# Head outputs return inside the last attention head, and the w_b and w_out stages are entered row by row (gMLP + latent attention + expert-choice block, one core)

## The reference

```
p = rmsnorm(x) @ w_in                     # u, v, c_q, c_kv, k_rope, gate_A, gate_B
a_out = chunked spatial gating of u, v, @ w_a_out
b_out = attention(q, k, v of 8 heads) @ w_b_out
x = x + (sigmoid(gate_A) * a_out + sigmoid(gate_B) * b_out) @ w_out
x = x + expert_choice_ffn(rmsnorm(x))     # 16 experts
```

## Time and profile before

| | |
|---|---|
| median of 3 runs | 2310.31 us (2306.19 to 2315.46) |
| the profiled execution | 2310.33 us, span 2308.6 us |
| mean granted TensorE clock | 0.97 of full speed |
| PE busy | 2136.6 us (93% of the span) |
| DVE, ACT, POOL busy | 1212.7, 921.9, 715.9 us |
| w_a tiles 6 and 7 | 759 to 803 us of the span |
| last head of attention | 1115 to 1168 us |
| w_b | 1179 to 1296 us |
| w_out | 1302 to about 1440 us |

### The profile page before, as it was taken

One profiled execution on the slowest core, in us unless ns is written; L12 is line 12 of the kernel. 1 busy time (PEld: TensorE's weight loads), 2 busy tenths in 40 slices (PEclk: granted clock), 3 DMA queues, 4 the chain that ended last, 5 costly groups with the idle time before them and its releaser, 6 DMA issues.

```text
span 2308.6 us, 34507 instructions
## 1 busy us (share of the span) xinstructions
PE 2136.6 (93%) x13812; PEld 1759.1 (76%) x13812; DVE 1212.7 (53%) x1395; ACT 921.9 (40%) x1156; POOL 715.9 (31%) x438
## 2 busy tenths in 40 slices
PE   6999999999989799999969899279999999999996
PEld 5887878888778678888868899257777777777774
DVE  5245402222566367776632413747676767777673
ACT  4112211111544266666520103135555555555552
POOL 3332312123255276666613320211212222122211
PEclk9999999999999999999989999589999999999998
DMA  4121223444567521321143411547888888878873
GB/s 146 53 85 67 93 85 125 142 154 161 197 228 246 191 67 62 91 77 60 34 187 96 157 30 78 214 180 267 291 293 288 287 295 291 294 286 283 296 287 110
DMA packets 189220, 396.85 MB, mean 172 GB/s; under 512 B 16208, under 2 KB 110416, under 8 KB 189136
## 3 DMA queue, kind: packets, MB, share of 16 engines
q1 hardware_dynamic: 176080, 343.25, 41.7%
q0 software_dynamic: 6144, 20.98, 4.2%
q10 hardware_dynamic: 6912, 31.46, 3.4%
HBM read 317.01 MB, written 78.64 MB: 171 GB/s over the span
## 4 chain that ended last, share of the span: by engine, by line
PE 84%; DVE 5%; ACT 3%; DMA 3%; issue 2%; POOL 2%; SPq 1%; ACTq 0%; DVEq 0%; POOLq 0%
PE PS L1229 24%; PE PS L341 13%; PE PS L343 13%; PE PS L342 13%; PE PS L1239 8%; PE PS L1087 2%; PE PS L1074 1%; PE PS L1078 1%; PE PS L1076 1%; PE PS L1075 1%; PE PS L1077 1%; PE PS L1021 1%; PE PS L1184 1%; ACT prob L1525 1%; PE PS L980 1%
## 5 line engine op out<-in xcount | busy, mean ns | idle before, releaser
L341 PE MATMUL PS<-act_hi,w_hi 128*128 128x512 f32 (+1 forms) x1248 | 452.6, 363 | 17.8 <-DVE act_lo L1724 11.2
L343 PE MATMUL PS<-act_hi,w_lo 128*128 128x512 f32 (+1 forms) x1248 | 446.3, 358 | 0.0
L342 PE MATMUL PS<-act_lo,w_hi 128*128 128x512 f32 (+1 forms) x1248 | 446.1, 357 | 0.0
L1983 DVE TENSOR_TENSOR elo<-raw,ehi 128x2048 fp32r<-128x2048 f32 x125 | 283.3, 2287 | 103.4 <-ACT ehi L1590 102.3
L1590 ACT ACTIVATE ehi<-raw 128x2048 fp32r<-128x2048 f32 x128 | 242.0, 1915 | 127.3 <-PE PS L1229 111.2
L341 PEld LDWEIGHTS PS<-act_hi,w_hi 128*128 128x128 f32 x1248 | 238.4, 191 | 51.3 <-issue 13.4
L343 PEld LDWEIGHTS PS<-act_hi,w_lo 128*128 128x128 f32 x1248 | 238.0, 191 | 34.6
L342 PEld LDWEIGHTS PS<-act_lo,w_hi 128*128 128x128 f32 x1248 | 238.5, 191 | 31.9
L785 POOL TENSOR_SCALAR prob<-prob,small 128x1024 f32<-128x1024 f32 (+1 forms) x80 | 196.9, 2462 | 134.4 <-DVE small L1852 134.4
L684 POOL TENSOR_SCALAR w_hi<-w_raw 128x1024 fp32r<-128x1024 f32 x52 | 57.8, 1111 | 500.6 <-PE PS L343 464.3
L835 POOL DMA_INDIRECT y_p<-ob_p,ixs_p x16 | 44.6, 2785 | 454.0 <-DVE ob_s L2027 454.0
(11 more groups left out here) (265 smaller groups left out, 4236.4 us busy)
## 6 DMA issues: line engine op xcount, KB each, us to landing
raw<-in_w_up SPq DMA_DIRECT2D x62, 1024.0 KB, 5.7
raw<-in_w_gate SPq DMA_DIRECT2D x34, 1024.0 KB, 4.9
raw_more<-in_w_down SPq DMA_DIRECT2D x32, 1024.0 KB, 7.6
raw<-in_w_down SPq DMA_DIRECT2D x32, 1024.0 KB, 6.3
raw_more<-in_w_gate SPq DMA_DIRECT2D x30, 1024.0 KB, 5.9
...
```

Of the source, the lines that this page charges most:

```text
L341: pe.matmul(out, lh, rh, start=first, stop=False)
L342: pe.matmul(out, lh, rl, start=False, stop=False)
L343: return pe.matmul(out, ll, rh, start=False, stop=last)
L1983: dve.tensor_tensor(elo[:, pt], raws[slot], f32(ehi[:, pt]), ALU.subtract).then_inc(S["e_lo"], 1)
```

## The change

1. `head_piece`: the first head's 9 pieces start at position 14 of w_a tile 6 instead of 2, and stand 3 instead of 4 positions apart. PE, ACT and DVE follow.
2. `o_all` and `z_all` go; `o_hl` holds both halves of the eight head outputs, in the room of the even heads' buffers. In the last head SP loads one output row a step (`load_o`, from step 71) into the two buffers `stg`, ACT rounds the high half (`o_part`, steps 72 to 77), and DVE subtracts the low half (steps 72 to 77). Rows 6 and 7 follow after step 83, row 7 behind the last pair's store.
3. `b_row`: the products of w_b tile 0 with rows 0 and 1 stand on PE in steps 80 and 81. The other 14 row products of tiles 0 and 1 follow after step 83. Tiles 2 to 7 wait block by block.
4. z tile by tile: SP loads `za_d[i]` into `stg` (`load_za`, in its queue behind the weights of w_b tile i and ahead of those of tile i+1). DVE adds, ACT rounds, and DVE subtracts each row right after its tile (`z_part`); row 0 comes after the gates of tiles 0 and 1.
5. w_out: PE starts with the banks 6 and 7 and takes the rest as they are evacuated. POOL splits the second weight tile in four pieces of two rows each. x is loaded after w_b's last product, since its room is now that of `o_hl`; the weights of the second quarter stand behind it on SP.

The diff, cut to the parts of which the prediction speaks:

```diff
-    q = 24 * (i - 6) + s - 2
-    return q // 4 if q >= 0 and q % 4 == 0 and q // 4 < PIECES else None
+    q = 24 * (i - 6) + s - 14
+    return q // 3 if q >= 0 and q % 3 == 0 and q // 3 < PIECES else None
...
-                o_all = sb(s2, "o_all", [P, KD, T])
-                z_all = sb(s2, "z_all", [P, KD, T])
+                o_hl = sb(s2, "o_hl", [P, KD, 2, T], F32R)
...
+            def load_o(k):
+
+                for r in range(2):
+                    sp.wait_ge(o_st[r], 16 * max(15, (5 * k + 5 + 1 - r) // 2))
+                    if k < 2:
+                        sp.wait_ge(stored[r], 16 * 20)
+                if k > 1:
+                    sp.wait_ge(S["part_lo"], at("part_lo", KD + k - 1))
+                sp.dma_start(stg[:, k % 2, :], o_d[k]).then_inc(ld_in[k % 2], 16)
...
-                if n == STEPS - NCH + 8:
-                    sp.wait_ge(S["scores_pe"], STEPS - NCH + 1)
-                    for r in range(2):
-                        sp.wait_ge(o_st[r], 16 * 15)
-                    sp.dma_start(o_all[:, 0:H - 2], o_d[0:H - 2].rearrange("h p t -> p h t")).then_inc(S["o_back"], 16)
+                if n > STEPS - NCH and n - (STEPS - NCH + 1) < H - 2:
+                    load_o(n - (STEPS - NCH + 1))
+            load_o(H - 2)
             store_values(5 * H - 1)
-            for r in range(2):
-                sp.wait_ge(o_st[r], 16 * 20)
-            sp.wait_ge(S["probT_pe"], STEPS)
-            for h in (H - 2, H - 1):
-                sp.dma_start(o_all[:, h], o_d[h]).then_inc(S["o_back_last"], 16)
+            load_o(H - 1)
...
+            def load_za(i):
+                j = i % 2
+                sp.wait_ge(S["part_lo"], at("part_lo", KD + (i + KD - 1)))
+                sp.dma_start(stg[:, j, :], za_d[i]).then_inc(ld_in[j], 16)
+                if i > 1:
+                    sp.wait_ge(S["z_sum"], at("z_sum", i - 1))
+                    sp.dma_start(gt[:, j, :], g_d[KD + i]).then_inc(gt_in[j], 16)
+
             for j in range(2):
                 sp.wait_ge(stored[j], 16 * 20)
-            for n, (k0, k1) in enumerate(((0, 2), (2, KD))):
-                sp.dma_start(z_all[:, k0:k1], za_d[k0:k1].rearrange("k p t -> p k t")).then_inc(S[f"za_in{n}"], 16)
-            with sp.Fori(1, KD // 2) as i:
-                for j in range(2):
-                    load_w(G_B + 2 * i + j, j, w_tile("b", 2 * i + j))
-                    sp.wait_ge(S["z_sum"], at("z_sum", 2 * i + (j - 1)))
-                    sp.dma_start(gt[:, j, :], g_d[2 * i + (KD + j)]).then_inc(gt_in[j], 16)
-
-
-            sp.wait_ge(S["part_lo"], at("part_lo", 2 * KD))
+            for i in range(2):
+                load_za(i)
+            for i in range(2, KD):
+                load_w(G_B + i, i % 2, w_tile("b", i))
+                load_za(i)
+            for j in range(2):
+                load_w(G_OUT + j, j, w_tile("o", j))
+            sp.wait_ge(S["tile_pe"], 3 * G_OUT)
...
-                    pool.wait_ge(S["part_lo"], at("part_lo", 3 * KD))
+                    pool.wait_ge(S["tile_pe"], 3 * G_OUT)
...
-                    settled()
-                    pool.tensor_scalar(wh[:, j], w_raw[:, j], 1.0, 0.0, ALU.mult, ALU.add).then_inc(S["w_rounded"], 1)
-                    pool.wait_ge(S["w_rounded"], g + 1)
-                    pool.tensor_tensor(wl[:, j], w_raw[:, j], f32(wh[:, j]), ALU.subtract).then_inc(S["w_split"], 1)
+                    for k in (range(0, KD, 2) if g == G_OUT + 1 else (0,)):
+                        ks = slice(k, k + 2) if g == G_OUT + 1 else slice(0, KD)
+                        hi = pool.tensor_scalar(wh[:, j, ks], w_raw[:, j, ks], 1.0, 0.0, ALU.mult, ALU.add)
+                        hi.then_inc(S["w_part"], 1)
+                        pool.wait_ge(S["w_part"], 2 * (q * 2 + j + 1 + (3 if g > G_OUT + 1 else k // 2)) - 1)
+                        pool.tensor_tensor(wl[:, j, ks], w_raw[:, j, ks], f32(wh[:, j, ks]), ALU.subtract)\
+                            .then_inc(S["w_part"], 1)
+                    pool.wait_ge(S["w_part"], 2 * (q * 2 + j + 1 + (3 if g > G_OUT else 0)))
+                    pool.sem_inc(S["w_split"], 1)
...
+            def b_row(j, k):
+
+                if k == 0:
+                    pe.wait_ge(S["w_split"], G_B + j + 1)
+                    pe.wait_ge(S["exp_act"], STEPS)
+                    if j == 1:
+                        pe.wait_ge(S["pt_lo_dve"], STEPS)
+                pe.wait_ge(S["part_lo"], at("part_lo", KD + k + 1))
+                for b, (t0, tn) in enumerate(BLOCKS):
+                    last = mm3(pe, lin_set(j, b), w_hi[:, j, k], w_lo[:, j, k], o_hl[:, k, 0, t0:t0 + tn],
+                               o_hl[:, k, 1, t0:t0 + tn], k == 0, k == KD - 1)
+                    if k == KD - 1:
+                        last.then_inc(S["tile_pe"], 1)
...
+                if n in (STEPS, STEPS + 1):
+                    b_row(0, n - STEPS)
...
+            for k in range(KD):
                 for j in range(2):
-                    pe.wait_ge(S["w_split"], g0 + j + 1)
-                    pe.wait_ge(S["evac"], 3 * (g0 + j - 1))
-                for k in range(KD):
-                    pe.wait_ge(S["part_lo"], at("part_lo", n0 + k + 1))
-                    for j in range(2):
-                        for b, (t0, tn) in enumerate(BLOCKS):
-                            last = mm3(pe, lin_set(j, b), w_hi[:, j, k], w_lo[:, j, k],
-                                       act_hi[:, k, t0:t0 + tn], act_lo[:, k, t0:t0 + tn], k == 0, k == KD - 1)
-                            if k == KD - 1:
-                                last.then_inc(S["tile_pe"], 1)
-                with pe.Fori(1, KD // 2) as i:
-                    for j in range(2):
-                        lin(g0 + 2 * i + j, j)
-
-            lin_split(G_B, KD)
-
-
-
-
+                    if j == 1 or k > 1:
+                        b_row(j, k)
...
-            pe.wait_ge(S["w_split"], G_OUT + 2)
-            pe.wait_ge(S["evac"], 3 * G_OUT)
+            pe.wait_ge(S["w_split"], G_OUT + 1)
             for k in range(KD):
                 pe.wait_ge(S["part_lo"], at("part_lo", 2 * KD + k + 1))
-                for c in range(8):
+                if k % 2 == 0:
+                    pe.wait_ge(S["w_part"], 2 * (k // 2 + 2))
+                for c in (6, 7, 0, 1, 2, 3, 4, 5):
+                    if k == 0:
+                        if c == 6:
+                            pe.wait_ge(S["values_act"], 5 * H)
+                        if c == 0:
+                            pe.wait_ge(S["evac"], 3 * G_OUT - 3)
+                        if c == 3:
+                            pe.wait_ge(S["evac"], 3 * G_OUT)
...
+            def o_part(k):
+                if k == 3:
+                    act.wait_ge(S["values_pe"], 5 * (H - 1))
+                    act.wait_ge(S["v_lo_pool"], H)
+                if k == H - 2:
+                    act.wait_ge(S["probT_pe"], STEPS)
+                act.wait_ge(ld_in[k % 2], 16 * (KD // 2 + k // 2 + 1))
+                act.activation(o_hl[:, k, 0], stg[:, k % 2, :], ACT.Copy).then_inc(S["part_hi"], 1)
...
+                if n - (STEPS - NCH + 2) in range(H - 2):
+                    o_part(n - (STEPS - NCH + 2))
+            o_part(H - 2)
             out_pair(5 * H - 1)
-
-            act.wait_ge(S["o_back"], 16)
-            act.wait_ge(S["o_back_last"], 32)
-            with act.Fori(0, H) as h:
-                act.activation(act_hi[:, h, :], o_all[:, h, :], ACT.Copy).then_inc(S["part_hi"], 1)
-            act.wait_ge(S["tile_pe"], 3 * G_OUT)
-            with act.Fori(0, KD) as k:
-                act.wait_ge(S["z_sum"], at("z_sum", k + 1))
-                act.activation(act_hi[:, k, :], z_all[:, k, :], ACT.Copy).then_inc(S["part_hi"], 1)
+            o_part(H - 1)
...
+                dve.tensor_tensor(o_hl[:, k, 1], stg[:, k % 2, :], f32(o_hl[:, k, 0]),
+                                  ALU.subtract).then_inc(S["part_lo"], 1)
...
+            def z_part(i):
+                j = i % 2
+                dve.wait_ge(ld_in[j], 16 * (KD + i // 2 + 1))
+                dve.wait_ge(S["evac"], 3 * (G_B + i + 1))
+                dve.tensor_tensor(stg[:, j, :], stg[:, j, :], gt[:, j, :], ALU.add).then_inc(S["z_sum"], 1)
+                dve.wait_ge(S["part_hi"], 2 * KD + i + 1)
+                dve.tensor_tensor(act_lo[:, i, :], stg[:, j, :], f32(act_hi[:, i, :]),
+                                  ALU.subtract).then_inc(S["part_lo"], 1)```

Three places show what moved. On DVE, steps 72 and 73 of the last head, before (L1837 and L1839 maximum and bias, L1846 low half of the probabilities, L1852 reciprocal):

```order
L1837 TENSOR_REDUCE small<-PS 128x1
L1839 TENSOR_SCALAR small<-small,rq 128x1
L1846 TENSOR_TENSOR pt_lo<-PS,pt_hi 128x8x128
L1852 RECIPROCAL small<-small 128x1
L1837 TENSOR_REDUCE small<-PS 128x1
L1839 TENSOR_SCALAR small<-small,rq 128x1
L1846 TENSOR_TENSOR pt_lo<-PS,pt_hi 128x8x128
L1852 RECIPROCAL small<-small 128x1
```

76 lines of the change are left out of this document (44 added, 32 removed).

## The result

| | before | changed |
|---|---|---|
| median | 2309.36 us | 2284.43 us (2281.06 to 2288.65) |
| ratio to before, 95% interval | | 0.9894 [0.9879, 0.9908] |
| the profiled execution | 2310.33, span 2308.6 | 2286.53, span 2284.8 |
| PE, DVE, ACT, POOL busy | 2136.6, 1212.7, 921.9, 715.9 | 2131.5, 1212.4, 923.0, 723.7 |

What follows compares the result with a forecast made beforehand. PE, busy 93% of the span, was taken as the bound, so gains come only where it stands still. Terms -8.2 + 1.0 - 1.1 - 3.3 - 0.6 = -12.2 us gave 2298.1 us, range 2287 to 2307.

Steps and rivals of the forecast that it cites:

- The loop: Last head: exponential, ACT's high half, DVE's low half, next maximum, next exponential; 7.35 us per full step with POOL blocking DVE.
- the rival without a block: Last head: POOL's normalisation does not hold DVE's low half; full step 5.3 us, six steps 28.9, total 2289; chance 0.17.
- the charge of 3.2 us for the lower clock: Last head and w_b rows: 3.2 us added for PE's lower granted clock after idling in lengthened steps.
- part 2: Heads' outputs handled inside the last head, through w_b tiles 0 and 1: +1.0 us, ends -9 to +9.
- 38.2: Forecast us for the last head's six steps with a returned row, block included; they took 24.2 before.
- The wait of 2.11 us: PE idle between the last head's last turns; row 0 of w_b tile 0 before them was to add only 0.3 us.
- The clock rival: Clock stays low through the last head's lengthened steps: 8 to 10 us where 3 was charged, about 2305; chance 0.18.
- the "slower" one: Lower clock lasts through the last head's steps and into 14 w_b rows: 2329 us; chance 0.03.
- part 1: Head 0's turns 12 positions later: 2.0 of the 10.26 us wait for the query load stay, -8.2 us.
- the wait of 11.17 us: PE idle from the last head's end to the first w_b product; forecast to go, with rows ready in time.
- -1.1 at tile 2: w_b tile 2: PE's 3.18 us wait for `w_lo` shortens by 1.1 us, as DVE's addition now comes behind `w_lo`.
- the 2.9 us before w_out: Start of w_out: PE's wait falls from 6.27 to 2.9 us, -3.3, if DVE's last addition beats POOL's quarter `w_lo`.

Runs made afterwards that it cites:

- experiment 4: Not the layer: POOL and VectorE operations alone and in pairs; VectorE's low half, 1.43 us alone, took 3.20 and 3.65 us beside POOL's two-input forms.
- experiment 3: Changed kernel with POOL's normalisation in the last head's last eight steps as a two-input product; 2286.68 us, ratio 0.9895.
- experiment 5: Not the layer: POOL operation paired with VectorE's low half started 0.15 to 1.1 us behind it; hold by the 1024-column normalisation ended 1.03 us after POOL's start.
- the second trace: The changed kernel run again with nothing altered, beside a version with three further edits on one chip; 2285.88 us, ratio 0.989.

## Why the prediction was wrong, and where it was right

**The step that failed** is the one that priced the low half: "Each keeps the other out whole. In the last head POOL normalises for 2.85 us a step, and starts before the low half is ready, so the low half waits for its end." The rows behind it were those of POOL's two-input subtraction. For that form the sentence is right (experiment 4: 3.65 us; experiment 3, the other two-input form: held to within 0.1 us of POOL's end in this very place). The normalisation reads one tensor, and it holds VectorE for the first 1.03 of its 2.85 us (experiment 5). Since the low half starts 0.91 us behind it, 0.12 us of hold were left. The loop without the block is 1.18 + 1.17 + 1.41 + 1.47 + 0.1 = 5.3, with 0.12 it is 5.45, and 5.45 to 5.47 were measured. So it was the rival without a block, given 0.17, that came true but for this 0.12 us. Its time of 2289 was still 4.6 us too long, for it kept the charge of 3.2 us for the lower clock. The page that the prediction cited, the Trainium skill, "SBUF — State Buffer", section "SBUF: two separate sides", says that whichever starts first has the port for the whole instruction. Experiments 4 and 5 agree where POOL was the one held (2.85 became 4.20 behind a low half of 1.43), and nearly for POOL's two-input forms (the hold ends at 1.81 of 1.89); they do not for the one-input forms (1.03 of 2.85, 0.95 of 2.77), and there the measurement decides.

The trace of before had a hint: POOL's high half of a weight, of as many columns, takes 1.05 us (L684, median) where the normalisation takes 2.85, so the busy time of the one needn't be its reading time. That was reason to doubt the price, not to know it. No row of before has this pair, and the block should have been measured, or priced from 1.05 to 2.85.

**The size of the miss**: part 2 was forecast at +1.0 and came to -8.7, 9.7 us off. 38.2 - 29.8 = 8.4 of it are the block, and 3.2 the charge for the lower clock, which was not there. 1.5 and 0.4 go the other way. The first is the tail: from the exponential of step 78 to the end of the last head's products it is 17.33 us (1148.33 to 1165.66) and was 15.53 (1152.28 to 1167.81), 1.8 more where I took 0.3. The wait of 2.11 us before the turns stayed, because row 0 stands behind it and not in it, and I had put the time of row 1 at nothing:

```profile
1161.04 0.40 PE L340 MATMUL PS<-o_hl,w_hi 128*128 128x512 f32 x1
...
1162.78 0.28 PE L340 MATMUL PS<-pt_hi,v_hi 128*128 128x256 f32 x1
...
1165.66 0.40 PE L340 MATMUL PS<-o_hl,w_hi 128*128 128x512 f32 x1
```

Row 1 takes from 1161.04 to 1162.78. The 0.4 are the other 14 rows, 24.5 us (1165.66 to 1190.18) for 24.1. Neither shows in the total, since the larger ones cover them. In the changed kernel's lengthened steps and in the w_b rows the windows show 1.00; only 1150 to 1160 show 0.84 and 0.82, behind the wait of 2.11 us that was there before. The clock rival falls with this, and the "slower" one, which needed 33 us of rows at the lower clock.

**Right**: part 1 (8.2 forecast, 7.0 to 7.9 in the mean of eight traces, though the lower clock behind the turn, which I had left as it was, is gone in some of them and not in others); that the rows arrive in time and the wait of 11.17 us vanishes; -1.1 at tile 2 (measured -1.19); the 2.9 us before w_out, for the reason given:

```profile
1277.05 1.49 DVE L1915 TENSOR_TENSOR stg<-stg,gt 128x1280 f32<-128x1280 f32 x1
```

```profile
1277.14 1.99 POOL L824 TENSOR_TENSOR w_lo<-w_raw,w_hi 128x256 fp32r<-128x256 f32 x1
```

VectorE's addition was there 0.09 us earlier, and POOL's quarter took 1.99 us. Tile 3's wait of 1.08 (1.77 in the second trace) lay in the range "0 to 2" of which I took 0. x and the weights behind it were in time, with 0.2 us of wait in all.

**Open**: a normalisation that really holds VectorE for 2.85 us wasn't tried, so that the sum as forecast has no run of its own; experiment 3 goes a part of that way (0.78 us more a full step for 0.77 more of low half). Part 2 was not run alone either. Nor is it settled what decides whether the clock falls behind a wait of 2.6 to 3.7 us, what moves the start of w_a tile 6 by 5 us between executions, or why the part behind w_out's start is 0.8 to 4 us shorter in all versions with the change.
